# A decoder step on one core: three token mixings moved among the products, a table load moved ahead of the output projection, and the first output turn moved among the last products

## The reference

```python
def sgu_mixer(h, w_in, sgu_g, w_s, b_s, w_out):
    z = jax.nn.gelu(h @ w_in, approximate=False)
    u, v = jnp.split(z, 2, axis=-1)
    v = rms_norm(v, sgu_g)
    ...
    s = jnp.einsum('gts,ncsgd->nctgd', wm, vp) + b_s[:, :cl].T[:, :, None]   # token mixing in chunks of 128
    return (u * s) @ w_out, v

def run_group(x, ...):
    m = sgu_mixer(...) or mla_mixer(...)          # layer A, layer B
    x = x + rms_norm(m, post_mix_g)
    f = conv_ffn(rms_norm(x, pre_ffn_g), ...)     # (gelu(g) * u) @ w_down
    x = x + rms_norm(f, post_ffn_g)
```

## Time and profile before

| | |
|---|---|
| median of 3 runs | 1406.64 us (1406.42 to 1407.43) |
| the profiled execution | 1406.9 us, its span 1405.0 us |
| PE busy | 1377.2 us, 98% |
| DVE, ACT, POOL busy | 890.7, 538.3, 176.0 us |
| granted TensorE clock, mean | 0.997 |
| DMA | 138.23 MB, mean 98 GB/s |

### The profile page before, as it was taken

The page is one execution under the profiler, slowest core; times in us unless marked ns, Lnnn a source line. Parts: engine busy times, 40 slices in busy tenths (PEclk is TensorE's granted clock), DMA queues, the critical chain, the costliest instruction groups (busy, mean ns, idle before and its releaser), DMA issues.

```text
span 1405.0 us, 30551 instructions
## 1 busy us (share of the span) xinstructions
PE 1377.2 (98%) x11843; PEld 1302.8 (93%) x11843; DVE 890.7 (63%) x1518; ACT 538.3 (38%) x882; POOL 176.0 (13%) x339
## 2 busy tenths in 40 slices
PE   8999999999999999999999989999999999999998
PEld 7999999999999999999999955559999999999998
DVE  5544665327888888733376587674678888884334
ACT  6445444226322222333375132544632222223334
POOL 2000000000222222110001120100022222221000
PEclk9999999999999999999999999999999999999999
DMA  7432222332233333233333574201323333323322
GB/s 230 120 90 76 76 75 76 92 90 76 85 95 90 90 90 92 66 100 91 95 103 109 207 280 176 76 1 46 91 76 90 93 95 95 91 67 89 94 86 77
DMA packets 224443, 138.23 MB, mean 98 GB/s; under 512 B 12710, under 2 KB 220742, under 8 KB 223328
## 3 DMA queue, kind: packets, MB, share of 16 engines
q1 hardware_dynamic: 219672, 112.36, 27.9%
q0 software_dynamic: 4512, 24.69, 4.6%
q10 hardware_dynamic: 184, 0.13, 0.0%
HBM read 133.84 MB, written 3.67 MB: 98 GB/s over the span
## 4 chain that ended last, share of the span: by engine, by line
PE 93%; DVE 3%; ACT 2%; issue 1%; DMA 0%; ACTq 0%; DVEq 0%
PE psum L701 80%; PE psum L1136 2%; PE psum L1268 1%; PE psum L1293 1%; PE psum L1097 1%; PE psum L900 1%; PE psum L1119 1%; DVE kt L2207 1%; PE psum L1271 1%; PE psum L886 0%; PE psum L1282 0%; PE psum L767 0%; DMA xs<-in_x_prompt 0%; PE psum L838 0%; ACT wh L1352 0%
## 5 line engine op out<-in xcount | busy, mean ns | idle before, releaser
L1825 DVE TENSOR_TENSOR wl<-ws,wh 128x1024 fp32r<-128x1024 f32 x211 | 258.4, 1225 | 310.5 <-ACT wh L1355 174.7
L701 PE MATMUL psum<-xh,wh 128*128 128x260 f32 x2000 | 410.0, 284 | 3.3 <-DVE xl L1844 1.9
L701 PE MATMUL psum<-xh,wl 128*128 128x260 f32 x2000 | 407.6, 284 | 0.0
L701 PE MATMUL psum<-xl,wh 128*128 128x260 f32 x2000 | 406.8, 283 | 0.0
L701 PEld LDWEIGHTS psum<-xh,wh 128*128 128x128 f32 x2000 | 310.7, 189 | 4.6 <-issue 2.1
L701 PEld LDWEIGHTS psum<-xh,wl 128*128 128x128 f32 x2000 | 310.8, 189 | 0.0
L701 PEld LDWEIGHTS psum<-xl,wh 128*128 128x128 f32 x2000 | 309.8, 189 | 0.0
L1355 ACT ACTIVATE wh<-ws 128x1024 fp32r<-128x1024 f32 x144 | 152.0, 1056 | 298.1 <-PE psum L701 298.1
L701 PE MATMUL psum<-acth,wh 128*128 128x260 f32 x704 | 147.6, 284 | 0.6 <-DVE wl L1825 0.6
L701 PE MATMUL psum<-acth,wl 128*128 128x260 f32 x704 | 146.2, 283 | 0.0
L701 PE MATMUL psum<-actl,wh 128*128 128x260 f32 x704 | 146.1, 282 | 0.0
(11 more groups left out here) (317 smaller groups left out, 1843.9 us busy)
## 6 DMA issues: line engine op xcount, KB each, us to landing
ws<-in_w_up SPq DMA_DIRECT2D x88, 512.0 KB, 3.8
ws<-in_w_in_a SPq DMA_DIRECT2D x32, 512.0 KB, 4.1
ws<-in_w_down SPq DMA_DIRECT2D x30, 384.0 KB, 3.3
ws<-in_w_down SPq DMA_DIRECT2D x28, 320.0 KB, 3.1
ws<-in_w_out_a SPq DMA_DIRECT2D x16, 512.0 KB, 3.9
ws<-in_w_o SPq DMA_DIRECT2D x8, 512.0 KB, 4.7
xn<-in_x_prompt SPq DMA_DIRECT2D x4, 512.0 KB, 7.7
ws<-in_w_dq SPq DMA_DIRECT2D x4, 512.0 KB, 6.4
```

Source lines behind the costliest of these rows:

```text
L701: mm = pe.matmul(psum[:, 2 * slot + b, 0:HB], w, r[:, k, b * HB:(b + 1) * HB], start=st, stop=en)
L1825: dve.tensor_tensor(low_, ws[:, slot4, :], f32(high), ALU.subtract).then_inc(w_low, 1)
```

## The change

Four things. In the gate stage PE's first three token mixings, each now with the turn of the next tile behind it, take later places: `mix(0)` with `turn_values(1)` goes from ahead of block 5 of unit 1 to ahead of block 1 of unit 2; `mix(1)` with `turn_values(2)` goes from between units 1 and 2 (the turn: ahead of block 5 of unit 2) to ahead of block 6 of unit 2; `mix(2)` with `turn_values(3)` goes from between units 2 and 3 to ahead of block 3 of unit 3. In the update behind the attention, `roots()` is issued ahead of the weight splits of the output projection instead of in the update. At the end the first turn (h = 0, g = 0) is issued behind the block before the last of the last unit, its copy on ACT lies ahead of the squares of the last tile's second half, and of the dummy matmuls those ahead of turns 1 to 3 of h = 1 are gone while the six ahead of turn 0 no longer wait for `y_ready`. The semaphore `qz_clear` is split in two, and POOL waits for its own memset.

```diff
-            pool.memset(qz[:, 0:QB // 2, :, :], 0.0).then_inc(qz_clear, 1)
+            pool.memset(qz[:, 0:QB // 2, :, :], 0.0).then_inc(qz_zero_p, 1)
+            pool.wait_ge(qz_zero_p, 1)
...
                             if h and (i, kk) == (0, 1):
                                 half_rms(name, 0)
+                            if name == "m_ffn1" and (h, i, kk) == (1, 1, len(ks) - 2):
+                                turn_out(0, 0)
...
-            WARM = (6, 2, 2, 2)
...
-            def mix_early():
-                mix(0, 0)
-                turn_values(1)
+            def mix_then_turn(j):
+                mix(j, j // 2)
+                turn_values(j + 1)
...
-            gate_unit(1, 1, {2: turn_roots, 5: mix_early})
-            mix(1, 0)
-            gate_unit(2, 2, {5: lambda: turn_values(2)})
-            mix(2, 1)
-            turn_values(3)
-            gate_unit(3, 3)
+            gate_unit(1, 1, {2: turn_roots})
+            gate_unit(2, 2, {1: lambda: mix_then_turn(0), 6: lambda: mix_then_turn(1)})
+            gate_unit(3, 3, {3: lambda: mix_then_turn(2)})
             mix(3, 1)
...
+            def turn_out(h, g):
+
+                if h:
+                    pe.wait_ge(y_ready, g + 1)
+                pe.wait_ge(m_ready, MB["m_ffn1"] + KD + (h or g == 3))
+                pe.wait_ge(x_new, 6 * KD + KD * h + 2 * g + 2)
...
             for h in range(2):
                 for g in range(4):
-                    if h:
-                        pe.wait_ge(y_ready, g + 1)
-                        for _ in range(WARM[g]):
+                    if (h, g) == (1, 0):
+                        for _ in range(6):
                             pe.matmul(psum[:, 6, 0:P], ones[:, :], ones[:, :], start=True, stop=True)
...
+                    if h or g:
+                        turn_out(h, g)
...
-                roots()
                 if p == 3:
                     sq_slot_free(name, KD - 2)
                     sixth(0)
+                else:
+                    roots()
                 sq_slot_free(name, KD - 1)
                 last_square(0)
                 rms(name, r2, 0)
                 last_raw(0)
                 if p == 4:
+                    out_rows(0, 0)
                     last_square(1)
...
             for sent in okn_sent:
                 act.wait_ge(sent, 32)
+            roots()
             for t in range(KD):
                 ahead_static(U_O + t)
```

More of the change, by code:

```diff
@@ L368, in trunk @@
         csT_done, csn_ready, csn_sent, m_ready = S("csT_done"), S("csn_ready"), S("csn_sent"), S("m_ready")
-        evac_kv, evac_dq, evac_uq, rotk_done, rotk_step, ck_step, ckt_ready = (S(n) for n in (
-            "evac_kv", "evac_dq", "evac_uq", "rotk_done", "rotk_step", "ck_step", "ckt_ready"))
+        evac_kv, evac_dq, evac_uq, rotk_done, rotk_step, qz_zero_p, ckt_ready = (S(n) for n in (
+            "evac_kv", "evac_dq", "evac_uq", "rotk_done", "rotk_step", "qz_zero_p", "ckt_ready"))
         cqh_ready, cql_ready, rotq_done, rotq_step = (S(n) for n in (
@@ L375, in trunk @@
             "ql_read", "qlT_done", "ols_ready", "olpT_done", "oss_ready", "osT_done", "own_low", "narrow_clear"))
-        ukT_done, ukt_ready, ql_done, qsel_done, qz_clear, qz_v, qz_a, qown_ready, so_done, so_ready, sn_done, sn_ready, zpad = (S(n) for n in (
-            "ukT_done", "ukt_ready", "ql_done", "qsel_done", "qz_clear", "qz_v", "qz_a", "qown_ready", "so_done", "so_ready", "sn_done", "sn_ready", "zpad"))
+        ukT_done, ukt_ready, ql_done, qsel_done, qz_zero_a, qz_v, qz_a, qown_ready, so_done, so_ready, sn_done, sn_ready, zpad = (S(n) for n in (
+            "ukT_done", "ukt_ready", "ql_done", "qsel_done", "qz_zero_a", "qz_v", "qz_a", "qown_ready", "so_done", "so_ready", "sn_done", "sn_ready", "zpad"))
         kv_done, kv_read_a, kv_read_v, nT_done, n_ready, n_sent = (S(n) for n in (
@@ L974, in _ @@
                 wo_tile(3, e)
+            def turn_out(h, g):
[3 more added lines that the diff above has]
+                pe.wait_ge(x_new, 6 * KD + KD * h + 2 * g + 2)
+                for e in range(2):
+                    for c in range(2):
+                        mm = pe.transpose(psum[:, g, (2 * e + c) * P:(2 * e + c + 1) * P], x[:, 2 * g + e, (2 * h + c) * P:(2 * h + c + 1) * P], ident)
+                mm.then_inc(yT_done, 1)
+                if h:
+                    for e in range(2):
+                        mm = pe.transpose(psum[0:NS, 4 + g // 2, (2 * (g % 2) + e) * P:(2 * (g % 2) + e + 1) * P], x[:, 2 * g + e, SEQ:T], ident)
+                    if g % 2:
+                        mm.then_inc(ysT_done, 1)
             def mlp(l):
@@ L1390, in square, with out_rows @@
                 act.activation(halves(out) if len(src.shape) == 3 else out, src, ACT.Square).then_inc(sq_done, 1)
+            def out_rows(h, g):
+                act.wait_ge(yT_done, 4 * h + g + 1)
+                act.activation(yn[:, 2 * h:2 * h + 2, 2 * g * P:2 * (g + 1) * P].rearrange("p c (e f) -> p e c f", e=2),
+                               psum[:, g, :].rearrange("p (e c f) -> p e c f", e=2, c=2), ACT.Copy).then_inc(y_ready, 1)
             def update(p, name, m, ahead_of_norm):
@@ L1682, in _ @@
             half_qz = QB // 2 * NS * 32
-            act.activation(qz[:, QB // 2:, :, :].rearrange("p a b c -> p (a b c)"), cst[:, 0:half_qz], ACT.Copy, scale=0.0).then_inc(qz_clear, 1)
+            act.activation(qz[:, QB // 2:, :, :].rearrange("p a b c -> p (a b c)"), cst[:, 0:half_qz], ACT.Copy, scale=0.0).then_inc(qz_zero_a, 1)
             act.wait_ge(ql_done, 1)
             act.activation(turn[:, :], psum[:, 2, :], ACT.Copy).then_inc(ql_read, 1)
-            act.wait_ge(qz_clear, 2)
+            act.wait_ge(qz_zero_a, 1)
+            act.wait_ge(qz_zero_p, 1)
             act.wait_ge(qsel_done, 1)
@@ L1808, in _ @@
                 for g in range(4):
-                    act.wait_ge(yT_done, 4 * h + g + 1)
-                    act.activation(yn[:, 2 * h:2 * h + 2, 2 * g * P:2 * (g + 1) * P].rearrange("p c (e f) -> p e c f", e=2),
-                                   psum[:, g, :].rearrange("p (e c f) -> p e c f", e=2, c=2), ACT.Copy).then_inc(y_ready, 1)
+                    if h or g:
+                        out_rows(h, g)
                     if (h, g) == (1, 1):
@@ L2212, in _ @@
             turn_keys(0, 0)
-            dve.wait_ge(qz_clear, 2)
+            dve.wait_ge(qz_zero_a, 1)
+            dve.wait_ge(qz_zero_p, 1)
             dve.wait_ge(qsel_done, 1)
```

## The result

The changed kernel takes **1409.21 us** (median, 1408.11 to 1410.25), the kernel before 1406.59 beside it (1405.89 to 1408.6; 19 runs of each). The ratio is 1.0017 [1.0011, 1.0023]: 2.6 us slower, just inside the 0.2% that the prediction drew as its bound. The profiled execution of the changed kernel is its fastest, 1408.11 us with a span of 1406.2; the one of before took 1406.9 with a span of 1405.0. So the spans differ by 1.2 us where the medians differ by 2.6, and the profile has to be read place by place. One run of the kernel before, out of the 27 beside the last group of experiments, took 2025.4 us at a granted clock of 0.619; the ratios leave it out, and the medians hardly see it.

What follows compares the result with a forecast made beforehand. PE was taken as the bound, busy 98% of the span, with the gate stage starting as a chain through ACT and DVE. 2.37 - 0.19 + 0.35 = +2.53 us on the median 1406.64 gave 1409.2 us, range 1408.1 to 1410.1.

Steps and rivals of the forecast that it cites:

- `turn_values(1)` later: Gate stage: the turn behind the first mixing starts at 129.46 instead of 126.26, 3.20 us later.
- restart of unit 2, PE's stands: Gate stage: one PE stand of 1.7 us turns into stands of 0.2, 1.4, 1.0 and 1.2 us.
- gate stage: The three moved mixings make this stage 2.37 us later, bounds 2.2 to 2.7, and it isn't given back.
- table load: Output projection: load moved into ACT's idle time; sum of squares starts 0.19 us earlier, bounds 0.1 to 0.25.
- end: Last turns and output DMAs: 0.35 us later in sum, bounds 0 to 0.7.
- semaphores: Split of `qz_clear`: costs nothing; at most a gather 0.15 us late, covered by several microseconds.
- the relay: Gate stage: ACT and DVE steps from `normalized(1)` to `normalized(3)` without slack, passing on the first turn's 3.20 us delay.
- The cap by DVE's two splits: Output projection: two weight splits ahead of DVE's `sixth_squares` limit the table load's gain to 0.19 us, not 1.28.
- The second case: End: the first transfer's leaving early shortens the third's issue, so the fourth ends 0.2 us later instead of 0.5.
- A: Rival: the gate stage's delay doesn't arrive, leaving -0.19 + 0.35, 1406.8 us; chance 0.10.
- B: Rival: mixings find inputs ready, PE's 1.70 us gate-stage stand goes with no new one, 1405.1 us; chance 0.07.
- C: Rival: TensorE's clock falls at the end once dummy matmuls are gone, +0.66 us, 1409.9 us; chance 0.07.

Runs made afterwards that it cites:

- the mixings alone: Only the three mixings moved as in the change, against the kernel before: 1418.03 us against 1415.58; G, the roots' turn to the fifth mixing, 31.61 us.
- its own experiment: Only the end changed (first turn moved, dummy matmuls ahead of the last three turns gone), against the kernel before: 1416.13 us, +0.55 us, ratio 1.0002.
- three kernels: Three kernels without the last three turns' dummy matmuls, first turn unmoved: one otherwise as before (1416.08 us against 1415.96), two with other edits (1414.27 and 1414.04 us).
- the kernel with the second mixing three blocks forward: Second and third mixings moved, second ahead of unit 2's block 3; Gelu's and roots' tables loaded earlier, last three turns' dummies gone; against before: 1414.04 us against 1416.41.

## Why the prediction was right

Forecast 1409.2, measured 1409.21 us; +2.53 us by the sum, +2.62 by the medians.

| step | forecast, us | measured, us |
|---|---|---|
| `turn_values(1)` later | 3.20 | 3.19 (129.35 + 0.10 of earlier start, against 126.26) |
| restart of unit 2, PE's stands | 0.2, 1.4, 1.0, 1.2 | 0.2, 1.26, 0.87, 1.05 |
| gate stage | +2.37 | +2.37 (G of the mixings alone: 31.61 - 29.24) |
| table load | -0.19 | -0.18 (0.81 to 0.63) |
| end | +0.35, 0 to 0.7 | +0.22 to the prompt's last bytes (its own experiment 0.24), +0.25 to the end of the span against the experiments' 12.09 (its own experiment 0.27), but -0.03 against before's 12.37 |
| semaphores | 0 | nothing that can be told (+0.08 in the kernel with the mixings of before) |

**The mixings.** The step that carried the result was that the relay has no slack from `normalized(1)` on. It held to 0.01 us over three pieces 16 us apart. The stands came out 0.14 us shorter each than forecast while the starts behind them came as forecast: the idle time in brackets begins at the modelled end of the last matmul, which lies behind its start by the tail of the pipeline, while I had reckoned from the time at which the next could have started. Forecasts of starts are the ones to compare.

**The table load.** The cap by DVE's two splits held; 0.18 us, not the load's 1.28. DVE's sum starts as its splits end. Behind them ACT still has a part: the split of `w_up` ahead of the two waits 0.19 us for ACT's copy, in before as in after, so the remaining 0.63 us are DVE's and ACT's work on weights and not DVE's alone.

**The end.** The mechanism was right in every row (DVE's half 0.57 late for 0.58, the last turn 0.13 for 0.16). The term was sized too large, by 0.08 to 0.13 us against the experiments' kernels: the forecast has 0.16 us for the last turn and 0.19, the middle of its two cases, for the transfers behind it. They took 3.15 us instead of 3.03, 0.12 more. The second case, in which the early first transfer eases the later ones, is the nearer. The pause that the forecast put ahead of turn (1, 0), 0.9 us, came as 0.52 us there and 0.94 us ahead of (1, 2).

**The semaphores.** The gather behind POOL's memset begins after 0.27 us of idle time instead of 0.15, so 0.12 us later; the forecast had at most 0.15 and nothing of it arriving.

**What agreed by luck.** The forecast stood on one execution 0.3 us above its median. The profile of after is 1.1 us below its own. Between the two profiles of the first pair the sum of the three terms is 2.37 - 0.18 + 0.22 = 2.41, and the spans differ by only 1.2. The missing 1.2 us has three parts. 0.10 is the earlier start of the gate stage. 0.25 is the end: the sum takes +0.22 for it, while from the last sum to the end of the span these two executions differ by -0.03 (12.34 and 12.37 us), before's being slower there than all others that leave the end alone (12.09). And 0.84 falls in the sample attention. The changed kernel's offset is 2.20 us at PE's products of 815 us and 1.36 at those of 871. 0.47 of it goes where before's execution has one row of 16 matmuls at 848.83 that lasts 1.11 us, against 0.64 in the changed kernel; the rest at a pause of before's that the trace puts down to nothing:

```profile
856.48 1.06 PE L1097 MATMUL psum<-kt,qz 128*32 128x128 f32 x27 [0.76 <-issue]
```

and the changed kernel's, 1.8 us later in its span, has this:

```profile
858.25 0.65 PE L1112 MATMUL psum<-kt,qz 128*32 128x128 f32 x16 [0.23 <-DVE kt L2221]
```

What PE waits at that line, for `kt` and for nothing shown, sums to 5.0 us in the changed kernel's profile and 5.5 in before's, and in those of the experiments, on the other chips, to 5.9 to 6.8 us, whichever edit they have. The change does touch this stage, by the split of `qz_clear`. But the changed kernel with the mixings of before, which has the split, waits 6.4 us there, and the ten other experiments, which don't have it, lie on both sides of that. I take it for scatter of that stage between executions, which no experiment was made to test. A forecast built on one execution can miss by such an amount; the terms as measured sum to 2.4 us, the forecast is 2.53, the medians differ by 2.62 in an interval of 1.5 to 3.2: the agreement to 0.01 us is chance, the one to a few tenths is not.

**The rivals.** A (the delay doesn't arrive, 0.10) and B (the stands go, 0.07) fall by the mixings alone. C (the clock, 0.07) falls by the windows. The forecast's range, 1408.1 to 1410.1, holds the median; it also holds 18 of the 19 single runs. By its own terms (1.95 to 3.3 us and 0.3 for scatter) it should have read 1408.3 to 1410.2, which holds the median too. The chances stood with 0.62 on "within 0.2%" and 0.36 on slower; the interval of the ratio, 1.0011 to 1.0023, lies on both sides of that bound too, and it leaves out a ratio of 1. Slower it is; by how little, was the forecast.

## What to carry to other kernels

When several engines hand each other tiles in order, the first hand-over sets every later one: look up which idle time on the side engine the moved instruction ends, and move only those that have cover. Here the first of three moves cost 3.2 us (2.37 + 0.82) and the two others gained 0.8. A table load belongs in the idle time ahead of the chain, not at its first user inside of it, and was worth its own time there (1.40 us); where another engine's work is late anyway, as at the output projection, it is worth only the difference to that. When a stand is gone, ask what the timeline shows as late next, and move that one. And at the end of a kernel count up to the end of the span: the last turn without its dummies came 0.46 us earlier, and in the mean of three kernels the span ended no earlier.

## What the runs showed of the hardware that was not expected

One kernel, the one before, takes 1406.6 us beside the changed kernel and 1415.6 to 1416.4 us on the three chips of the experiments, with a mean granted clock of 0.995 to 0.999 in every profile. 3.5 us of it is one wait of PE for DVE's `qown`, 0.6 us in both profiles of the first pair and 4.0 to 4.2 in those of the experiments. In the waits of the kernel with the second mixing three blocks forward it reads:

```profile
PE psum L1169 <- DVE qown L2224: 4.1, 1, 4.1
```

What makes that wait, and the other 5 us or so, was not found. Unexpected too was that PE's stream of small matmuls (128 x 32 weights, 128 columns) loses between 5.9 and 6.8 us to waits on those chips, one execution and the next, with no edit in it: a spread of 0.9 us, as much as most of the effects looked for here. And TensorE's clock read 1.00 up to the last turn with the dummy matmuls gone.
